# Large tiles at multiples of 2048 bytes in a partition of SBUF

## The chip, the cores and the metric

One NeuronCore of a Trainium2 chip runs the whole program in one launch. The metric is device time in microseconds. The kernel before takes 2143.19 us, the median of 3 runs (2142.52 to 2144.78). PE is TensorE, ACT is ScalarE, DVE is VectorE, POOL is GpSimd, SP is the engine that issues nearly all DMAs.

## The reference

The input is one sequence of 512 tokens of width 1024 and a context of 256 tokens, all in float32. A first block modulates both with adaptive layer norms (six vectors from `silu(c) @ w_ada`), multiplies by `w_in`, runs a bidirectional state space scan, a Fourier mix and a pooling mix, and multiplies by `w_out`. A feed-forward part follows:

```python
a = dwconv2d_grid(h @ w_up, conv_w, conv_b)      # w_up 1024 x 5632
val, gate = jnp.split(a, 2, axis=-1)
return (jax.nn.gelu(gate) * val) @ w_down        # w_down 2816 x 1024
```

Then come two hybrid layers. Each projects the normed stream (`w_in`), runs an attention over the best 256 keys of an indexer and a stabilised mLSTM, multiplies by `w_out`, and ends with

```python
u = rms_norm(h, g_mlp) @ w_ff1                   # 1024 x 4096
h = h + jnp.square(jax.nn.relu(u)) @ w_ff2       # 4096 x 1024
gate = jax.nn.sigmoid(rms_norm(h, g_ple) @ w_ple_gate + b_ple_gate)
return h + gate * (p_i @ w_ple)
```

## The kernel before, in words

**Layout.** Activations lie with features on the 128 partitions and tokens along the partition: a tile of 1024 features is 8 pieces of 512 float32, so 8 times 2048 bytes, 16,384 bytes in a partition. `h` is the residual stream, `mix` holds 8 working pieces, and `ring` has two slots of one weight tile each (1024 x 256, 8 pieces of 1024 bytes).

**Products.** A product is made at float32 accuracy from three matmuls in the float32r type. Each operand is held as a high and a low part: `xh`, `xl` for the activations that come out of a norm, `acts` for both parts of the activations inside the feed-forward parts (`U1`, `n.U`), of the input of `w_out_2` and of the gate projection, `ctxr` for the context, `wh`, `wl` for the weights. `product` (lines 794 to 796) and `part` (811 to 813) loop over the 8 pieces k of 128 contraction rows and issue `hi x hi`, `hi x lo`, `lo x hi`: stationary a 128x128 piece of `wh` or `wl` (512 bytes in a partition, the two halves of a tile 512 bytes apart, consecutive k 1024 bytes apart), moving a 128x512 piece of the activations. Every matmul loads its own weights first. `product_t` (828 to 830) turns it round: stationary a piece of `xh` or `xl`, moving 256 or 80 columns of `wh` or `wl`. All other matmuls (transposes, sums, Fourier, `w_ple`, attention) are in plain float32.

**Weights.** SP loads each tile into `ring` (line 741); ACT writes the high part into `wh` (line 1428), and DVE (1958) or POOL (2783) writes `ring - wh` into `wl`. The matmuls of a half wait for its low part. The order of all this in the mixers stands in the hand-written tables `MIXER` and `LAYER`; in the feed-forward parts the loops `up1`, `down1`, `up2`, `down2` set it. None of it depends on where a tile lies.

**Places.** `sb` opens an SBUF tensor; the allocator gives addresses in the order of the calls. The first tile begins at byte 1152 of each partition, and each later one at the next multiple of 32 after the one before it. So in the kernel before:

```
tile                         start (bytes)        past a multiple of 2048 / of 512
h                            1152                 1152 / 128
xh, xl                       17536, 33920         1152 / 128
wh, wl                       50304, 66688         1152 / 128
mix, ring                    83072, 99456         1152 / 128
small ones (con ... turn)    115840 to 133072     various
arena, acts, arena_f/m0/m1   133088 (the base)    2016 / 480
acts00, acts10 (n.U)         145376               2016 / 480
early                        172000               2016 / 480
ctxr, arena2                 198048               1440 / 416
```

The tiles from the base on overlap one another in time (they are opened and closed in `with` blocks): `arena` serves the first mixer, `acts` its feed-forward part, `arena_m` the mixer of a layer, `acts00` and so on its feed-forward part. `ahead` is opened only to push `early`, the landing place of seven weight tiles for the adaptive norm, above what the first norms use.

Of the kernel before, what the change touches and what calls it, by code (L numbers as in the profile page):

```python
# [9 lines left out]
I32 = mybir.dt.int32  # L10
# [21 lines left out]
def const_layout():  # L32
    names = [("ident", 128), ("ule", 128), ("uge", 128), ("ugt", 128), ("ult", 128), ("ones", 128),
             ("mean", 128), ("neg", 128), ("pen", 128), ("freq", 8), ("sel", 16), ("pair", 16), ("fold", 128)]
    at, n = {}, 0
    for name, w in names:
        at[name] = n
        n += w
    return at, n
# [57 lines left out]
def offsets(table):  # L97
    at, n = {}, 0
    for name, w in table:
        at[name] = n  # L100
        n += w
    return at, n
# [287 lines left out]
def build(nc, A, out):  # L390
    cat, cn = const_layout()
    pat, pn = offsets(PARAMS)
    rat, rn = offsets(ROWS)

    with ExitStack() as ctx:
        def sb(name, n, dt=F32, where=ctx):
            return where.enter_context(nc.sbuf_tensor(name, [128, n], dt))
# [8 lines left out]
        up, at, now = tally.up, tally.at, tally.now  # L406

        h_t, xh_t, xl_t = sb("h", 4096), sb("xh", 4096, F32R), sb("xl", 4096, F32R)
        wh_t, wl_t = sb("wh", 2 * SLOT, F32R), sb("wl", 2 * SLOT, F32R)  # L410
        mix_t, ring = sb("mix", 4096), sb("ring", NSLOT * SLOT)
        con, par, rb, mod = sb("con", cn), sb("par", pn), sb("rb", rn), sb("mod", 96)
        fw, pw, posi = sb("fw", 128), sb("pw", 128), sb("posi", 4, I32)
        rope, eps, csil_t, small = sb("rope", 64), sb("eps", 3), sb("csil", 256), sb("small", 1024)
        turn_t = sb("turn", 100)
        posf, ang, kk, rr = turn_t[:, 0:4], turn_t[:, 4:36], turn_t[:, 36:68], turn_t[:, 68:100]

        def by8(t):
# [3 lines left out]
        csil = csil_t[:, :].rearrange("p (k w) -> p k w", w=32)  # L422
# [48 lines left out]

        with ExitStack() as low:
            sb("ahead", 9728, where=low)
            early_t = sb("early", 7 * SLOT, where=low)
        early = {i: early_t[:, n * SLOT:n * SLOT + SLOT].rearrange("p (k n) -> p k n", k=8) for n, i in enumerate((0, 1, 4, 5, 2, 6, 7))}

        with ExitStack() as low:
            cut = Cut(sb("arena", 16240, where=low), 16240)
            arow = [cut(512), cut(512)]  # L480
            con1 = cut(1280)
            part2 = con1[:, 0:512]
            m1 = cut.o
            hc = cut(2048).rearrange("p (j t) -> p j t", j=8)
            xc_ctx = cut(2048).rearrange("p (j t) -> p j t", j=8)
            sq1, rs1, rs2, part1 = [cut(512) for _ in range(4)], cut(512), cut(256), cut(512)
            assert cut.o <= 9728
            cut.o = m1
            Xt = cut(3072).rearrange("p (q n) -> p q n", q=6)
            Bt = cut(1536).rearrange("p (q n) -> p q n", q=6)  # L490
            Z_ = cut(2048)
            Z = Z_.rearrange("p (q n) -> p q n", q=4)
            fA = Z_.rearrange("p (c i s f) -> p c i s f", c=4, i=2, s=2)
            BT = cut(1024).rearrange("p (g t) -> p g t", g=2)
            CT = cut(1024).rearrange("p (g t) -> p g t", g=2)
            acc = [cut(512) for _ in range(4)]
            Ms = [cut(1024) for _ in range(3)]
            with ExitStack() as high:
                ctxr = sb("ctxr", 4096, F32R, where=high)
                ch = ctxr[:, 0:2048].rearrange("p (j t) -> p j t", j=8)  # L500
                cl = ctxr[:, 2048:4096].rearrange("p (j t) -> p j t", j=8)
            with ExitStack() as high:
                cut = Cut(sb("arena2", 4096, where=high), 4096)
                pb = [cut(2 * 544).rearrange("p (i t) -> p i t", i=2) for _ in range(3)]
                cut.o = 0
                Sf = cut(2048).rearrange("p (q n) -> p q n", q=4)
                Sb = cut(2048).rearrange("p (q n) -> p q n", q=4)
                cut = Cut(sb("arena3", 3072, where=high), 3072)
                Ms.append(cut(1024))
                Ex, dmb = [cut(512), cut(512)], cut(512)  # L510
                dts, dtw0 = cut(256).rearrange("p (k n) -> p k n", n=32), cut(256)
# [12 lines left out]
        with ExitStack() as low:  # L524
# [3 lines left out]
            cut = Cut(sb("arena_f", 3584, where=low), 3584)  # L528
# [18 lines left out]
        for l in range(2):  # L547
            n = Layer()
            layers.append(n)
            with ExitStack() as low:  # L550
                cut = Cut(sb(f"arena_m{l}", 23824, where=low), 23824)
# [8 lines left out]
            with ExitStack() as low:  # L560
                cut = Cut(sb(f"arena_f{l}", 3072, where=low), 3072)
# [4 lines left out]
                with ExitStack() as high:  # L566
                    cut = Cut(sb(f"arena_p{l}", 5120, where=high), 5120)
# [2368 lines left out]
```

## Time and profile before

| | |
|---|---|
| median of 3 runs | 2143.19 us |
| the profiled execution, its own time | 2150.59 us |
| its span, first to last instruction | 2148.6 us |
| mean granted clock of TensorE | 0.981 |
| PE busy | 2084.7 us, 97% of the span |
| DVE, ACT, POOL busy | 54%, 41%, 37% |
| matmuls | 10,284 |
| DMA | 90 GB/s over the span |

How to read it: busy matmuls overlap one another, since they are pipelined. The duration of one (0.39 us for 512 columns) is its way through the array, and a new one starts well before the last has ended. How fast TensorE works is read from the distance between the starts of successive matmuls in a timeline, here called the pitch. 512 columns at 2.4 GHz are 213.3 ns, 256 columns 106.7 ns.

### The profile page before, as it was taken

Reading aid. Unit: us, or ns where it says so; the run is one execution under the profiler, and the core shown is the slowest. Engines: PE = TensorE matmul, PEld = TensorE weight load, DVE = VectorE, ACT = ScalarE, POOL = GpSimd, SP = SyncE. Lnnn points to the kernel's source line nnn. Section 1 sums busy time; section 2 is a strip of 40 time slices with the busy share of each in tenths; the row PEclk is TensorE's granted clock in tenths of the full one; section 3 lists DMA queues with packets and bytes.
Section 4 is the critical chain, followed back from the end, with each engine's and each line's share of the span. In section 5 each row is a group of like instructions: output and inputs, shape, how many; then the busy total and the mean of one; then the engine's idle time right before and its main releaser. Section 6 shows DMA issues by size and latency. Waiting matters only on the chain. (4 is left out here: it accounts for less than half of the span.)

```text
span 2148.6 us, 25815 instructions
## 1 busy us (share of the span) xinstructions
PE 2084.7 (97%) x10284; PEld 1608.4 (75%) x10284; DVE 1162.4 (54%) x2013; ACT 882.6 (41%) x1391; POOL 787.9 (37%) x404
## 2 busy tenths in 40 slices
PE   6999999999999999999999999989999999999998
PEld 3877677888887877667888887677776788888866
DVE  5366759995574579954523121345997553123124
ACT  4543334442333566854322122336677432222132
POOL 0233115675563334420544444001434134444420
PEclk9999999999999899999999999999999999999999
DMA  9134631232222202112333322221111133332212
GB/s 314 58 99 157 196 98 42 96 118 98 88 99 75 79 1 79 40 59 79 108 98 98 98 98 92 65 85 40 60 59 40 61 100 105 98 98 88 95 53 98
DMA packets 186662, 194.23 MB, mean 90 GB/s; under 512 B 8496, under 2 KB 181936, under 8 KB 186160
## 3 DMA queue, kind: packets, MB, share of 16 engines
q1 hardware_dynamic: 184880, 187.35, 27.1%
q10 hardware_dynamic: 1664, 5.24, 0.7%
q8 instruction: 82, 1.34, 0.3%
q14 instruction: 36, 0.29, 0.0%
HBM read 190.48 MB, written 2.10 MB: 90 GB/s over the span
## 5 line engine op out<-in xcount | busy, mean ns | idle before, releaser
L2783 POOL TENSOR_TENSOR wl<-ring,wh 128x1024 fp32r<-128x1024 f32 (+1 forms) x252 | 619.1, 2461 | 905.7 <-ACT wh L1428 904.7
L1428 ACT ACTIVATE wh<-ring 128x1024 fp32r<-128x1024 f32 (+2 forms) x294 | 304.4, 1043 | 348.6 <-PE ps L796 265.2
L794 PE MATMUL ps<-xh,wh 128*128 128x512 f32 x960 | 377.0, 393 | 1.9 <-POOL wl L2783 1.7
L795 PE MATMUL ps<-xl,wh 128*128 128x512 f32 x960 | 374.4, 390 | 0.0
L796 PE MATMUL ps<-xh,wl 128*128 128x512 f32 x960 | 374.1, 390 | 0.0
L794 PE MATMUL ps<-acts,wh 128*128 128x512 f32 x880 | 348.5, 396 | 3.1 <-DVE wl L1958 3.1
L796 PE MATMUL ps<-acts,wl 128*128 128x512 f32 x880 | 350.5, 398 | 0.0
L795 PE MATMUL ps<-acts,wh 128*128 128x512 f32 x880 | 347.7, 395 | 0.0
L2425 DVE SCALAR_TENSOR_TENSOR mix<-ps,par,mix 128x441 f32<-128x441 f32 (+2 forms) x352 | 213.6, 688 | 30.2 <-ACT mix L1659 30.1
L794 PEld LDWEIGHTS ps<-xh,wh 128*128 128x128 f32 x960 | 180.5, 188 | 45.6 <-issue 7.8
L795 PEld LDWEIGHTS ps<-xl,wh 128*128 128x128 f32 x960 | 180.6, 188 | 37.8 <-issue 0.7
L796 PEld LDWEIGHTS ps<-xh,wl 128*128 128x128 f32 x960 | 180.6, 188 | 37.8
L794 PEld LDWEIGHTS ps<-acts,wh 128*128 128x128 f32 x880 | 165.6, 188 | 50.0 <-issue 10.8
L795 PEld LDWEIGHTS ps<-acts,wh 128*128 128x128 f32 x880 | 165.5, 188 | 42.3 <-issue 0.7
L796 PEld LDWEIGHTS ps<-acts,wl 128*128 128x128 f32 x880 | 165.5, 188 | 38.6
L2496 DVE TENSOR_TENSOR h<-h,ps 128x512 f32<-128x512 f32 x64 | 44.1, 689 | 274.5 <-PE ps L796 274.5
L1726 ACT ACTIVATE acts<-mix 128x512 fp32r<-128x512 f32 x64 | 40.5, 632 | 235.3 <-DVE mix L2484 235.3
L2484 DVE SCALAR_TENSOR_TENSOR mix<-ps,arena_f 128x512 f32<-128x512 f32 x64 | 44.2, 690 | 142.0 <-PE ps L796 142.0
L828 PE MATMUL ps<-wh,xh 128*128 128x256 f32 (+1 forms) x352 | 109.3, 310 | 1.4 <-ACT arena_m L1433 1.1
L830 PE MATMUL ps<-wh,xl 128*128 128x256 f32 (+1 forms) x352 | 106.1, 302 | 0.0
L829 PE MATMUL ps<-wl,xh 128*128 128x256 f32 (+1 forms) x352 | 106.0, 301 | 0.0
L811 PE MATMUL ps<-xh,wh 128*128 128x512 f32 x224 | 95.9, 428 | 0.0
(431 smaller groups left out, 3141.4 us busy)
## 6 DMA issues: line engine op xcount, KB each, us to landing
ring<-in_w_ff_dram SPq DMA_DIRECT2D x64, 1024.0 KB, 5.4
ring<-in_w_in_dram SPq DMA_DIRECT2D x28, 1024.0 KB, 5.4
ring<-in_ffn_w_up_dram SPq DMA_DIRECT2D x22, 1024.0 KB, 5.0
ring<-in_w_ada_dram SPq DMA_DIRECT2D x17, 1024.0 KB, 5.2
ring<-in_w_out_dram SPq DMA_DIRECT2D x12, 1024.0 KB, 5.2
ring<-in_ffn_w_down_dram SPq DMA_DIRECT2D x8, 1024.0 KB, 5.0
ring<-in_w_ple_gate_dram SPq DMA_DIRECT2D x8, 1024.0 KB, 5.3
early<-in_w_ada_dram SPq DMA_DIRECT2D x7, 1024.0 KB, 12.1
```

The costliest lines, as they stand in the source:

```text
L794: t.matmul(b[0:m, 0:n], s.hi[:, k, a:a + m], x2[0][:, k, :], start=k == ks[0], stop=False)
L795: t.matmul(b[0:m, 0:n], s.hi[:, k, a:a + m], x2[1][:, k, :], start=False, stop=False)
L796: i = t.matmul(b[0:m, 0:n], s.lo[:, k, a:a + m], x2[0][:, k, :], start=False, stop=k == ks[-1])
L811: t.matmul(b[:, :], s.hi[:, k, a:a + 128], x2[0][:, k, :], start=k == ks[0], stop=False)
L828: t.matmul(b[:, 0:s.w], x0[:, k, :], s.hi[:, k, 0:s.w], start=k == 0, stop=False)
L829: t.matmul(b[:, 0:s.w], x0[:, k, :], s.lo[:, k, 0:s.w], start=False, stop=False)
L830: i = t.matmul(b[:, 0:s.w], x1[:, k, :], s.hi[:, k, 0:s.w], start=False, stop=k == 7)
L1428: a.activation(s.hi[:, :, c], s.ap[:, :, c], ACT.Copy).then_inc(*up("hi", "hi", name, hf))
L2425: k = v.scalar_tensor_tensor(o, grid(ps(key)[:, :], dr, dc, True), pc("ffn_conv_w", w * 44 + col), o, ALU.mult, ALU.add)
L2484: v.scalar_tensor_tensor(u, ps(key)[:, :], 0.0, n.rs2, ALU.max, ALU.mult).then_inc(*free(key))
L2496: v.tensor_tensor(h[:, j, :], h[:, j, :], ps(key)[:, :], ALU.add).then_inc(*free(key))
L2783: p.tensor_tensor(s.lo[:, :, c], s.ap[:, :, c], s.hi[:, :, c].bitcast(F32), ALU.subtract).then_inc(*up("lo_pool", "lo", name, hf))
```

## The change

The small tiles are opened first and the seven large ones after them. `turn` grows from 100 to 108 elements, which makes the small ones end at byte 18,416, rounded to 18,432, 9 times 2048. The large ones end at 133,120, 65 times 2048. As `ahead` and the arena have 32 bytes less room above them, `rs2` (256 elements, the reciprocal root of the context's variance) no longer has a place of its own in the arena and uses the first 256 elements of `small`, whose users begin later; `ahead` shrinks by 256 elements.

```diff
+        con, par, rb, mod = sb("con", cn), sb("par", pn), sb("rb", rn), sb("mod", 96)
+        fw, pw, posi = sb("fw", 128), sb("pw", 128), sb("posi", 4, I32)
+        rope, eps, csil_t, small = sb("rope", 64), sb("eps", 3), sb("csil", 256), sb("small", 1024)
+        turn_t = sb("turn", 108)
         h_t, xh_t, xl_t = sb("h", 4096), sb("xh", 4096, F32R), sb("xl", 4096, F32R)
         wh_t, wl_t = sb("wh", 2 * SLOT, F32R), sb("wl", 2 * SLOT, F32R)
         mix_t, ring = sb("mix", 4096), sb("ring", NSLOT * SLOT)
-        con, par, rb, mod = sb("con", cn), sb("par", pn), sb("rb", rn), sb("mod", 96)
-        fw, pw, posi = sb("fw", 128), sb("pw", 128), sb("posi", 4, I32)
-        rope, eps, csil_t, small = sb("rope", 64), sb("eps", 3), sb("csil", 256), sb("small", 1024)
-        turn_t = sb("turn", 100)
...
-            sb("ahead", 9728, where=low)
+            sb("ahead", 9472, where=low)
...
-            sq1, rs1, rs2, part1 = [cut(512) for _ in range(4)], cut(512), cut(256), cut(512)
-            assert cut.o <= 9728
+            sq1, rs1, rs2, part1 = [cut(512) for _ in range(4)], cut(512), small[:, 0:256], cut(512)
+            assert cut.o <= 9472
```

The places after it:

```
tile                         start (bytes)        past a multiple of 2048 / of 512
small ones (con ... turn)    1152 to 18416        various
h, xh, xl, wh, wl, mix, ring 18432 to 133120      0 / 0
arena, acts, arena_f/m0/m1   133120 (the base)    0 / 0
acts00, acts10 (n.U)         145408               0 / 0
early                        171008               1024 / 0
ctxr, arena2                 198080               1472 / 448
```

The instructions, their order, their waits and their shapes stay as they are.

## Rows read from the trace of the kernel before

**Rows 1.** The head of the page and its busy times by engine

```profile
span 2148.6 us, 25815 instructions
PE 2084.7 (97%) x10284; PEld 1608.4 (75%) x10284; DVE 1162.4 (54%) x2013; ACT 882.6 (41%) x1391; POOL 787.9 (37%) x404
```

**Rows 2.** Windows: length, busy us of PE, PEld, DVE, ACT, POOL, clock, DMA share, GB/s

```profile
449.75:500.00 50.25, 50.25 (x223) 41.63 (x222) 46.81 (x79) 21.70 (x28) 34.52 (x20) 1.00 0.28 91
1100.00:1130.00 30.00, 30.00 (x130) 24.12 (x130) 4.14 (x6) 6.05 (x6) 12.01 (x5) 1.00 0.28 82
```

**Rows 3.** Timeline of PE (start, duration), `xh` moving: two matmuls 27 starts apart

```profile
449.75 0.39 PE L794 MATMUL ps<-xh,wh 128*128 128x512 f32 x1
...
455.87 0.39 PE L794 MATMUL ps<-xh,wh 128*128 128x512 f32 x1
```

**Rows 4.** The same with `acts` moving: two matmuls 27 starts apart

```profile
1099.59 0.39 PE L794 MATMUL ps<-acts,wh 128*128 128x512 f32 x1
...
1105.89 0.39 PE L794 MATMUL ps<-acts,wh 128*128 128x512 f32 x1
```

**Rows 5.** The same with `ctxr` moving, 256 columns: two matmuls 33 starts apart

```profile
107.53 0.28 PE L794 MATMUL ps<-ctxr,wh 128*128 128x256 f32 x1
...
111.38 0.28 PE L794 MATMUL ps<-ctxr,wh 128*128 128x256 f32 x1
```

**Rows 6.** The same with weights moving, 256 columns: two matmuls 8 starts apart

```profile
177.53 0.28 PE L829 MATMUL ps<-wl,xh 128*128 128x256 f32 x1
...
178.49 0.28 PE L828 MATMUL ps<-wh,xh 128*128 128x256 f32 x1
```

**Rows 7.** Chain of waits: 28 plain float32 matmuls of 512 columns in a row

```profile
2086.38 12.02 PE ps L1223 x28
```

**Rows 8.** Timeline of PE where `acts` gives way to `xh`: 9 starts apart

```profile
1724.22 0.40 PE L794 MATMUL ps<-xh,wh 128*128 128x512 f32 x1
...
1726.30 0.39 PE L794 MATMUL ps<-xh,wh 128*128 128x512 f32 x1
```

**Rows 9.** Groups by form: count, busy us, mean ns, idle before and its releaser

```profile
L794 PE MATMUL ps<-xh,wh 128*128 128x512 f32 x960 | 377.0, 393 | 1.9 <-POOL wl L2783 1.7 <-DVE wl L1958 0.2
L794 PE MATMUL ps<-acts,wh 128*128 128x512 f32 x880 | 348.5, 396 | 3.1 <-DVE wl L1958 3.1
L811 PE MATMUL ps<-xh,wh 128*128 128x512 f32 x224 | 95.9, 428 | 0.0
L811 PE MATMUL ps<-acts,wh 128*128 128x512 f32 x64 | 27.0, 421 | 4.6 <-DVE acts L2771 4.6
L828 PE MATMUL ps<-wh,xh 128*128 128x256 f32 x288 | 87.0, 302 | 1.4 <-ACT arena_m L1433 1.1
L794 PE MATMUL ps<-ctxr,wh 128*128 128x256 f32 x48 | 13.4, 279 | 0.0
```

**Rows 10.** Groups by form of DVE, ACT and POOL, on tiles at different places

```profile
L2484 DVE SCALAR_TENSOR_TENSOR mix<-ps,arena_f 128x512 f32<-128x512 f32 x64 | 44.2, 690 | 142.0 <-PE ps L796 142.0
L2496 DVE TENSOR_TENSOR h<-h,ps 128x512 f32<-128x512 f32 x64 | 44.1, 689 | 274.5 <-PE ps L796 274.5
L1726 ACT ACTIVATE acts<-mix 128x512 fp32r<-128x512 f32 x64 | 40.5, 632 | 235.3 <-DVE mix L2484 235.3
L1448 ACT ACTIVATE arena_f<-h 128x512 f32<-128x512 f32 x40 | 25.3, 632 | 124.1 <-DVE h L2471 53.1 <-DVE h L2496 49.2 <-PE ps L896 11.3
L2783 POOL TENSOR_TENSOR wl<-ring,wh 128x1024 fp32r<-128x1024 f32 x244 | 604.3, 2481 | 882.9 <-ACT wh L1428 881.9
```

**Rows 11.** Waits of PE: us in total, times, longest

```profile
PE ps L877 <- DMA h<-in_x_dram: 10.8, 2, 8.5
PE ps L811 <- DVE acts L2771: 4.6, 2, 2.3
```

**Rows 12.** DMA issues: queue, count, KB each, median us to landing

```profile
arena_m<-in_w_iq_up_dram ACTq DMA_DIRECT2D x2, 512.0 KB, 3.9
mix<-in_p_dram ACTq DMA_DIRECT2D x2, 512.0 KB, 3.6
```

## The prediction, made blind

> **What bounds the kernel now.** I read the page's busy times first. PE is busy for 2084.7 us of 2148.6, 97% [rows 1], so only what PE does faster, or the 64 us in which it does nothing, can move the end. The windows come next: in a stretch of an up projection and in one of a down projection PE has no gap at all and the full clock, while POOL is busy for 34.5 of 50.25 us and for 12.0 of 30 us and DMA runs at under 30% [rows 2]. There nothing is late but PE itself. But "busy" doesn't say how fast a busy PE works, so the third view is the timeline, and in it the distance between starts. That is where this case lies, because a change of addresses alters no instruction, no order and no wait; it can act only through what one instruction takes.
>
> With `xh` or `xl` moving, 27 starts lie 6.12 us apart: 226.7 ns each [rows 3]. With `acts` moving, the same instruction on the same shape with the same kind of weights takes 6.30 us for 27: 233.3 ns [rows 4]. The columns alone would need 213.3 ns. So each matmul pays 13.3 ns above its columns in the first case and 20.0 ns in the second. The windows say the same by counts: 223 starts in 50.25 us are 225 ns each, 130 in 30 us are 231 ns, each a little low because a started matmul at the edge counts in full [rows 2]. The two differ in what other engines do at the same time (DVE 93% busy beside the cheap one, 14% beside the dear one), and the dear one is the quiet one, so the difference isn't contention with DVE, ACT or POOL. What is left that tells them apart is the place of the moving tile: `xh` begins 1152 bytes past a multiple of 2048, as `wh` and `wl` do, `acts` 2016 bytes past one.
>
> Three more rows fix how far that reasoning goes. Plain float32 matmuls of 512 columns take 12.02/28 = 429.3 ns [rows 7]; that is twice 213.3 and 2.6 ns, although these too load new weights each time. So plain float32 pays nothing for its place, and the extra is a matter of the float32r matmuls. With weights moving and `xh` stationary, 256 columns take 0.96/8 = 120.0 ns [rows 6], again 13.3 ns above the columns; there both tiles lie 1152 past, the roles are swapped and the length is halved, and the extra is the same. With `ctxr` moving, 1440 past, against `wh`, 256 columns take 3.85/33 = 116.7 ns [rows 5], an extra of 10.0 ns. So the extra is 13.3 where moving and stationary tile lie equally (0 bytes apart modulo 512), 20.0 at 352 apart and 10.0 at 288 apart. Within a stretch it does not change from k to k or half to half, though the stationary piece then steps by 512 and by 1024 bytes: whatever it depends on repeats every 512 bytes. I take this as a conflict between reading the moving operand and loading the next weights, which depends on how the two lie to one another.
>
> **The change part by part.** *The large tiles.* After the change `acts` and `wh`, `wl` lie 0 apart, as `xh` and `wh` do today, so the 233.3 ns should become 226.7 ns, 6.67 ns less. How many: 880 at each of three lines and 64 at each of three more, 944 x 3 = 2832 [rows 9]. 2832 x 6.67 ns = 18.9 us. All of them but a few stand where PE has no gap: the down projections, the gate projection and the second halves of `w_out_2`. The exception is the start of `w_out_2` in each layer, where PE waits for DVE's low parts, 4.6 us in two waits [rows 11]; of the first half's 48 matmuls per layer at most 96 x 6.67 ns = 0.6 us can vanish in such waits. I take off 0.2 us: 18.7 us. Where `acts` gives way to `xh` the first nine starts take 2.08 us and not 9 x 0.2267 = 2.04 [rows 8]; with both tiles alike this settling should go, five times 0.04 = 0.2 us (up after down, once in the first block and twice in each layer).
>
> *`xh`, `xl` against `wh`, `wl`*: both move by the same number of bytes, their relation stays, and I take 0. This is the largest unknown: (960 + 224) x 3 = 3552 matmuls of 512 columns and at least 288 x 3 = 864 of 256 [rows 9]. From below, if the place 0 costs no more than a plain float32 matmul (2.6 ns), each gains 10.7 ns, 47 us. From above, if 0 costs what 2016 costs, each loses 6.67 ns, 29 us. I take 0 since the four offsets that pieces of `wh` have today (128, 640, 1152, 1664) all cost the same.
>
> *`ctxr`*: 48 x 3 = 144 matmuls [rows 9]; its relation to `wh` goes from 288 to 448, which no row shows. Between 2.6 and 20.0 ns of extra where it is 10.0 now: -1.1 to +1.4 us; I take 0, the present value.
>
> *DVE, ACT, POOL*: DVE takes 690 ns with `arena_f` (2016 past) and 689 with `h` (1152 past), ACT 632 ns whether it writes `acts` or `arena_f` [rows 10]. The place costs these nothing: 0. PE's faster down projections ask for half a weight tile every 24 x 0.2267 = 5.44 us instead of 5.60; POOL makes one in 2.48 us [rows 10], so this supply doesn't turn late.
>
> *DMA*: destinations move too. The only pair of one size at two places is 512 KB into `arena_m`, 3.9 us, and into `mix`, 3.6 us [rows 12], 8% apart. The one wait of PE for a DMA is that for `h` at the start, 10.8 us [rows 11], and 8% of it is 0.9 us, so -0.9 to +0.9 us; I take 0, as the two rows are of different moments. Elsewhere weights arrive ahead.
>
> *`rs2` in `small`, `ahead`, `turn`*: the same instructions on other addresses; 0. There is no new wait, so nothing can queue behind one.
>
> Sum: -18.7 - 0.2 = -18.9 us. The profiled execution itself took 2150.59 us, 7.4 above the median of the runs; the same difference on the median gives 2143.19 - 18.9 = 2124.3 us. If only the relation counts, what is left open is `ctxr`, the start and the 0.6 us at `w_out_2`: 2121 to 2128.
>
> The Trainium skill has a rule against all this. "TensorE: Matmul & The Clock Gate", in "What happens when you issue a matmul", says that PE reads the moving operand and the next weights through two independent ports, and that loading weights takes no read bandwidth from the running matmul. By it the pitch can't depend on how the tiles lie, and the sum would be 0. The trace agrees for plain float32 (2.6 ns of extra) and disagrees with it as a whole for float32r, where the extra takes three values. The same page of the Trainium skill, section "Back-to-back issue gap", gives N/2.4 + 2.5 ns, 215.8 for 512 columns; none of the float32r streams here reaches it, and by it the time would be that of the deep fall among the rivals.
>
> **The rivals.** *The place doesn't matter (the change doesn't do what it says).* `acts` is also the only moving tile of 512 columns that lies above byte 131,072, and it does so after the change too. If the 20.0 ns come from that, or from anything else about `acts`, its pitch stays at 233.3 and the time within 1 or 2 us of 2143. For it: `ctxr` is up there too, and 20.0 ns on 512 columns and 10.0 on 256 are the same share, 9.4%. Against it: `xh` passes byte 32,768 and `wh` byte 65,536 on the way through their pieces, and rows 3 stay even. By the port rule of the Trainium skill's "TensorE: Matmul & The Clock Gate", quoted above, the time would be this one too.
>
> *Everything falls to what plain float32 pays.* If starts at 0 take the whole conflict away, 4416 matmuls gain 10.7 ns and the 2832 of `acts` gain 17.4: 47 + 49 = 96 us, 2047 us. For it: the extra does vary, so it isn't a fixed cost of float32r. Against it: with equal places today it is 13.3, not 0, in both roles.
>
> *The other side: the absolute place counts, and 0 is a bad one.* No row has a tile at 0; the nearest place modulo 2048 is 2016, 32 bytes before it, and it is the dear one. If `xh` takes over its 6.67 ns and `acts` keeps it, 4416 x 6.67 = 29.5 us are lost: 2172.7 us. It turns into a loss from the point where `xh` and its like lose more than 18.9 us/4416 = 4.3 ns each. Against it: places 512 apart cost the same, so 1152 stands for 128, and 2016 for 480; 0 then lies between them; and `ctxr`, off the multiples of 64 as `acts` is, is the cheapest of all.
>
> *In between*: `acts` improves, to some other value than 226.7, or `xh` shifts by 1 or 2 ns: 2128 to 2139.
>
> **How the numbers follow.** My forecast 0.65; no effect 0.12; everything falls 0.08; slower 0.10; in between 0.05. About 0.2%, 4.3 us, is what a measurement of this kernel can tell from no change. Faster by more: 0.65 + 0.08 + 0.05 = 0.78; within: 0.12; slower: 0.10. The time is the forecast's, 2124.3. Its own range of 2121 to 2128 holds not quite 0.65, so the range for 8 in 10 reaches over the middle to the case of no effect: 2119 to 2145, which leaves out the deep fall and the loss.
>
> **What would show it.** In the timeline of the changed kernel, 27 starts with `acts` moving should lie 6.12 us apart, and the nine after a change from `acts` to `xh` 2.04; with `xh` still 6.12; with `wh` moving 0.96 for 8; plain float32 still 12.02 for 28. DVE, ACT and POOL rows keep their means. I'm wrong in the step "relation, not place" if the `xh` streams move at all, and wrong altogether if `acts` stays at 6.30. If the pitches come out as said and the time doesn't fall by 17 us or more, the gain went into waits, first at `w_out_2` and the norms, and PE's share of the span would show it.

## The result, and the profile after

The kernel after takes 2130.68 us (median of 4 executions, 2129.14 to 2133.61) against 2143.99 (4 executions of the kernel before, 2142.52 to 2145.05): ratio 0.994, 95% interval 0.9923 to 0.9957. It is 13.3 us faster. Three later series of 5 and 6 executions, each beside the kernel before on the same chip, gave 0.9927, 0.9931 and 0.9917. The forecast was 2124.3 with a range of 2119 to 2145; the result lies in that range, but above the 2121 to 2128 that the prediction gave if only the relation counts.

The head of the page of the kernel after, against [rows 1]:

```profile
span 2129.5 us, 25815 instructions
PE 2061.1 (97%) x10284; PEld 1602.8 (75%) x10284; DVE 1161.6 (55%) x2013; ACT 882.1 (41%) x1391; POOL 787.1 (37%) x404
```

The span is 19.1 us shorter and PE's busy time 23.6, while DVE, ACT and POOL stay within 1 us: less work for PE, and not less waiting. Some 4 us of this pair are no gain of the change: the profiled execution before had a mean granted clock of 0.981, the one after 0.983 (0.002 of 2140 us, an estimate). PE's idle time even rises, from 63.9 to 68.4 us; part of that is the one execution profiled, since in further traces the waits listed for PE come to 61.3 and 61.9 us before and to 62.1 to 62.4 after. As before, the pitch tells more than the busy time. First the windows, to be read against [rows 2] (length, busy us of PE, PEld, DVE, ACT, POOL, clock, DMA share, GB/s). The second is again a stretch of a down projection:

```profile
449.75:500.00 50.25, 50.25 (x224) 41.60 (x223) 45.67 (x76) 20.01 (x27) 34.17 (x19) 1.00 0.31 104
1092.00:1122.00 30.00, 30.00 (x134) 24.82 (x134) 3.91 (x6) 6.15 (x6) 13.79 (x6) 1.00 0.35 105
```

In 30 us PE now starts 134 matmuls with `acts`, not 130; in the stretch with `xh` it starts 224, for 223 before. The timeline of the kernel after, pairs of matmuls 27 starts apart, first `xh`, then `acts`; then 33 starts of `ctxr`, 20 starts with weights moving, and the 9 starts where `acts` gives way to `xh`, against [rows 3 to 6, 8]:

```profile
449.83 0.39 PE L794 MATMUL ps<-xh,wh 128*128 128x512 f32 x1
...
455.95 0.39 PE L794 MATMUL ps<-xh,wh 128*128 128x512 f32 x1
...
1092.26 0.39 PE L794 MATMUL ps<-acts,wh 128*128 128x512 f32 x1
...
1098.38 0.39 PE L794 MATMUL ps<-acts,wh 128*128 128x512 f32 x1
```

```profile
105.02 0.28 PE L794 MATMUL ps<-ctxr,wh 128*128 128x256 f32 x1
...
108.91 0.28 PE L794 MATMUL ps<-ctxr,wh 128*128 128x256 f32 x1
...
175.13 0.28 PE L829 MATMUL ps<-wl,xh 128*128 128x256 f32 x1
...
177.53 0.28 PE L828 MATMUL ps<-wh,xh 128*128 128x256 f32 x1
```

```profile
1711.66 0.39 PE L794 MATMUL ps<-xh,wh 128*128 128x512 f32 x1
...
1713.70 0.39 PE L794 MATMUL ps<-xh,wh 128*128 128x512 f32 x1
```

`xh`: 6.12/27 = 226.7 ns, unchanged. `acts`: 6.12/27 = 226.7, where it was 233.3 [rows 4]. `ctxr`: 3.89/33 = 117.9, where it was 116.7 [rows 5]. Weights moving: 2.40/20 = 120.0, unchanged. The change from `acts` to `xh`: 2.04 us for 9, without the settling of [rows 8]. The chain of waits of the kernel after shows the plain float32 stream at its old 12.02 us for 28 [rows 7]:

```profile
2068.57 12.02 PE ps L1223 x28
```

Groups by form (count, busy us, mean ns, idle before and its releaser), against [rows 9, 10]:

```profile
L794 PE MATMUL ps<-xh,wh 128*128 128x512 f32 x960 | 376.8, 392 | 1.9 <-POOL wl L2783 1.7 <-DVE wl L1958 0.2
L794 PE MATMUL ps<-acts,wh 128*128 128x512 f32 x880 | 345.3, 392 | 3.3 <-DVE wl L1958 3.3
L794 PE MATMUL ps<-ctxr,wh 128*128 128x256 f32 x48 | 13.5, 281 | 0.0
L2484 DVE SCALAR_TENSOR_TENSOR mix<-ps,arena_f 128x512 f32<-128x512 f32 x64 | 44.2, 690 | 141.9 <-PE ps L796 141.8
```

The `acts` group is 3.2 us less busy and `xh`'s 0.2. Busy time of a group is no measure of the pitch, since the matmuls overlap, but it moves where the pitch does. Waits of PE (us in total, times, longest), against [rows 11]:

```profile
PE ps L877 <- DMA h<-in_x_dram: 10.8, 2, 8.6
PE ps L896 <- ACT arena_f L1448: 7.4, 4, 3.6
PE ps L811 <- DVE acts L2771: 4.6, 2, 2.3
```

The one wait that grows in every pair of traces is the middle one, PE for ACT's squares in the norms: 6.3 to 6.7 us in the kernels with slow `acts`, 7.2 to 7.8 in those with fast ones. Most of the growth stands around the gate projection of layer 0 (2.7 us before, 3.2 to 3.4 after), where PE now comes sooner and ACT doesn't. That gives back about 1 us.

The windows of the start, 14 to 38 us, of the kernel before and then of the kernel after (same columns as above), show what no step had foreseen:

```profile
14.00:38.00 24.00, 19.58 (x127) 7.20 (x127) 15.62 (x22) 14.96 (x29) 4.67 (x2) 1.00 1.10 342
```

```profile
14.00:38.00 24.00, 18.87 (x133) 7.24 (x130) 17.13 (x24) 15.45 (x30) 4.68 (x2) 1.00 1.09 380
```

At the same share of busy DMA engines 380 GB/s arrive, not 342. Issues of 1 MB into `ring` (the 64 of `w_ff`) land in 5.2 us, not 5.4, those into `early` in 10.8, not 12.1. Of [rows 12], the 512 KB into `mix` still take 3.6, and those into `arena_m` 4.2 where they took 3.9; but in the further traces these last take 4.2 before and 3.9 to 4.2 after, so that pair of rows is scatter.

### The profile page after: what moved, and what is told of

Its sections match the earlier page's. It is cut to its first block and busy times, and to the rows that moved or that the text cites. A ratio compares the mean times of both kernels' runs of the same rounds, so it can differ in the third digit from the quotient of the medians.

```text
span 2129.5 us, 25815 instructions
## 1 busy us (share of the span) xinstructions
PE 2061.1 (97%) x10284; PEld 1602.8 (75%) x10284; DVE 1161.6 (55%) x2013; ACT 882.1 (41%) x1391; POOL 787.1 (37%) x404
## 5 line engine op out<-in xcount | busy, mean ns | idle before, releaser
L794 PE MATMUL ps<-acts,wh 128*128 128x512 f32 x880 | 345.3, 392 | 3.3 <-DVE wl L1958 3.3
L796 PE MATMUL ps<-acts,wl 128*128 128x512 f32 x880 | 342.7, 389 | 0.0
L795 PE MATMUL ps<-acts,wh 128*128 128x512 f32 x880 | 342.6, 389 | 0.0
L794 PEld LDWEIGHTS ps<-acts,wh 128*128 128x128 f32 x880 | 165.4, 188 | 45.5 <-issue 11.6
## 6 DMA issues: line engine op xcount, KB each, us to landing
early<-in_w_ada_dram SPq DMA_DIRECT2D x7, 1024.0 KB, 10.8
```

Of the source, the lines that this page charges most:

```text
L794: t.matmul(b[0:m, 0:n], s.hi[:, k, a:a + m], x2[0][:, k, :], start=k == ks[0], stop=False)
L795: t.matmul(b[0:m, 0:n], s.hi[:, k, a:a + m], x2[1][:, k, :], start=False, stop=False)
L796: i = t.matmul(b[0:m, 0:n], s.lo[:, k, a:a + m], x2[0][:, k, :], start=False, stop=k == ks[-1])
```

## The experiments

### A map of the pitch by addresses

One kernel with nothing but streams of 24 matmuls, each line at another start of the moving tile (m) and the stationary one (s), counted in elements of 4 bytes in the code and in bytes in the text:

```diff
+for i in range(24): t.matmul(P[1][:, 0:512], W[:, s + 256 * (i % 8):s + 128 + 256 * (i % 8)],
+                             X[:, m + 512 * (i % 8):m + 512 + 512 * (i % 8)], start=i == 0, stop=i == 23)
```

> This kernel leaves the whole computation out and writes x back. It runs streams of 24 float32r matmuls, each stream on a line of its own, and varies only where the stationary piece begins (s bytes past a multiple of 2048) and where the moving piece begins (m bytes past one): 16 values of m in steps of 32 bytes with s = 0 and 512 columns; the same 16 differences m - s with s = 128; the same with s = 0 and 256 columns; m = 4 to 48 bytes; s = m = 4 to 256; plain float32 at m = 0, 32, 128. Before that, 4 MB are loaded in four DMAs of 1 MB to destinations 0, 32, 64, 128, 256 and again 0 bytes past a multiple of 2048. Theory 1, the relation counts: the 16 pitches with s = 0 and with s = 128 are the same row by row, 226.7 ns at difference 0 and 233.3 ns at 352 (480 against 128), 116.7 ns for 256 columns at 288, and s = m gives 226.7 at any value. Theory 2, the place of the moving tile alone counts: the row with s = 0 and the row with s = 128 agree by m and not by m - s; 233.3 at m = 480, 226.7 at m = 0 and 128, and 233.3 at s = m = 32. Plain float32 gives 429.3 ns everywhere by both. DMA: if the jump from 348 to 386 GB/s at the start is a matter of the destination, the groups at 0 and 256 run near 386 GB/s and those at 32, 64 and 128 near 348; if it isn't, all six are alike.

The chain of waits of this run (start, us, engine, line). Lines 152 to 167 are s = 0 and m = 0, 32, ..., 480 bytes; 168 and 169 the first two again with the stationary tile at 128; 184 to 191 are 256 columns at 0, 32, ..., 224 bytes:

```profile
119.11 5.44 PE ps L152 x24
124.55 5.60 PE ps L153 x24
130.16 5.50 PE ps L154 x24
...
163.69 5.47 PE ps L160 x24
...
208.29 5.48 PE ps L168 x24
213.77 5.60 PE ps L169 x24
...
297.50 2.87 PE ps L184 x24
300.37 2.83 PE ps L185 x24
...
314.57 2.73 PE ps L190 x24
...
409.47 20.60 PE ps L212 x48
```

A row's total divided by 24 is a little too high where the relation has just changed, since the first few starts of such a stream are slower (up to 236 ns in line 160, then 226.7). From the seventh start on the pitch is, by the distance of the moving start past the stationary one, to some 0.2 ns:

```
bytes past      0      32     64     96     128    160    192    224
512 columns     226.7  233.3  228.8  233.4  233.6  234.2  233.2  233.3   ns
256 columns     119.8  117.8  117.7  120.0  118.8  117.5  113.4  118.2   ns
```

The same run moved 4 MB by DMA to destinations 0, 32, 64, 128, 256 and again 0 bytes past a multiple of 2048 (windows of each group; the last column is GB/s):

```profile
22.18:34.00 11.82, 0.00 (x0) 0.00 (x0) 0.00 (x0) 0.00 (x0) 1.00 1.02 355
36.00:48.20 12.20, 0.00 (x0) 0.00 (x0) 0.00 (x0) 0.00 (x0) 1.00 1.03 333
...
64.00:76.70 12.70, 0.00 (x0) 0.00 (x0) 0.00 (x0) 0.00 (x0) 1.00 1.02 326
78.50:89.80 11.30, 0.00 (x0) 0.00 (x0) 0.00 (x0) 0.00 (x0) 1.00 1.02 362
```

Destinations on a multiple of 256 get 355 to 362 GB/s, those at 32, 64 and 128 get 326 to 333. From the first packet of a group to its last the trace has 11.6 to 11.8 us for the one kind and 12.6 to 12.8 for the other. That fits the faster start of the kernel after, whose `ring` and `early` came to multiples of 256. The rates that I had expected, 386 and 348, were those of a shorter stretch of the kernel's start.

### All large tiles at 2016, and the two kernels again

The kernel before, with four small tiles opened first and padded, so that `h`, `xh`, `xl`, `wh`, `wl`, `mix` and `ring` come to 2016 past a multiple of 2048, where `acts` lies: the relation of the kernel after, the dear place of the kernel before, and none of its DMA gain.

```diff
+        mod, turn_t, posi, eps = sb("mod", 96), sb("turn", 104), sb("posi", 8, I32)[:, 0:4], sb("eps", 8)[:, 0:3]
         h_t, xh_t, xl_t = sb("h", 4096), sb("xh", 4096, F32R), sb("xl", 4096, F32R)
...
-        con, par, rb, mod = sb("con", cn), sb("par", pn), sb("rb", rn), sb("mod", 96)
+        con, par, rb = sb("con", cn), sb("par", pn), sb("rb", rn)
```

> The kernel before with four small tiles (mod, turn, posi, eps: 864 bytes) opened ahead of the large ones and the rest behind them, so that xh, xl, wh, wl, mix and ring begin 2016 bytes past a multiple of 2048, where acts already is; the arena keeps its place at 133088. Nothing is at a multiple of 2048 and nothing at a multiple of 64. Theory 1, the relation of moving and stationary tile counts: acts falls from 233.3 to 226.7 ns, xh stays at 226.7, and the time is that of the changed kernel but for DMA. Theory 2, each tile's own place counts: acts stays at 233.3 and xh rises to 233.3 ns, 29 us slower than before, some 2172 us. DMA: by the destination theory the ring's and early's loads stay at the slower rate, 348 GB/s in the first 40 us.

> The changed kernel again, five rounds against the kernel before on the same chip. The trace shows 18.6 us less in the pitches of acts, but the medians lay only 13.3 us apart. If the profiled execution of before was merely one with more clock gating than usual, the ratio stays at 0.994; if the four runs of the first timing were unlucky, it goes to 0.9912 (18.9 us of 2143). Theory 1 for the missing 5 us: waits in the mixers between engines, which the trace after shows 3.7 us longer, are there in every execution.

> The kernel before again, for a second profile. If its first profiled execution (2150.6 us against a median of 2143.2) was one with more time at the lower clock, this one lies at 2143 to 2146 us with less time at it, and its pitches are 226.7 and 233.3 ns again.

Measured: 2133.36 us, ratio 0.9933 (0.9913 to 0.9953); beside it the kernel after 2131.67, 0.9927 (0.9909 to 0.9944). The one execution of the kernel before gave 2148.95, above the 2143 to 2146 expected, and its old pitches. The ratio of the kernel after, 0.9927, lies between the two values that its expectation had. Timeline of the shifted kernel, 27 starts apart, and its window of the start:

```profile
1094.00 0.39 PE L794 MATMUL ps<-acts,wh 128*128 128x512 f32 x1
...
1100.12 0.39 PE L794 MATMUL ps<-acts,wh 128*128 128x512 f32 x1
```

```profile
14.00:38.00 24.00, 19.60 (x126) 7.23 (x125) 15.62 (x22) 14.96 (x29) 4.66 (x2) 1.00 1.10 340
```

6.12/27 = 226.7 ns with everything at the place that I had called possibly bad, and 340 GB/s. Place 0 isn't needed, and the DMA rate isn't either: within the interval the whole gain comes without both. The rival "absolute place" falls.

### Only the relation of acts spoiled

The kernel after with 32 bytes in front of each `acts`, nothing else:

```diff
+            sb("gap_a", 8, where=low)
...
+                sb(f"gap_a{l}", 8, where=low)
```

> The changed kernel with eight elements (32 bytes) opened ahead of acts, acts00 and acts10, so that these lie 32 bytes past a multiple of 2048 and all else stays where the change put it, the DMAs' destinations too. By the relation theory acts goes back to 233.4 ns (the map's row at difference 32) and xh stays at 226.7; the time is 18.7 us above that of the changed kernel on the same chip. If the shortfall of the measured gain against the pitches is something that the faster acts brings with it, this kernel is only some 15 us slower; if it comes from the other tiles' new places, this kernel is the full 18.7 us slower and lies 3 us above the kernel before.

> The changed kernel again, for the comparison with the one above on the same chip and for more executions: a ratio of 0.9927, and at equal granted clock 17.5 us below the kernel before.

> The kernel before against itself: a ratio of 1.000, whose interval shows what five rounds can tell. Its executions scatter over 10 us with the granted clock, 2143 to 2145 us at 0.985 and 2148 at 0.984. If the mean clock of the executions is 0.9845 here and 0.983 for the changed kernel, the missing 2 to 4 us lie in the clock and not in the work.

Measured: 2145.79 us, ratio 0.9997 (0.9988 to 1.0007); beside it the kernel after 2131.8, 0.9931 (0.9917 to 0.9946), and the kernel before against itself 1.0001 (0.9988 to 1.0015). Timeline and start window of the spoiled kernel, whose line 796 is line 794 of the others:

```profile
1094.07 0.39 PE L796 MATMUL ps<-acts,wh 128*128 128x512 f32 x1
...
1100.36 0.40 PE L796 MATMUL ps<-acts,wh 128*128 128x512 f32 x1
```

```profile
14.00:38.00 24.00, 18.86 (x135) 7.40 (x131) 17.29 (x25) 15.29 (x30) 4.67 (x2) 1.00 1.10 381
```

6.29/27 = 233 ns, and the gain is gone altogether, with the DMA at its fast 381 GB/s. With the run before it this is a table of two by two: fast `acts` and slow DMA give 0.9933, slow `acts` and fast DMA give 0.9997. The change is worth what the relation of `acts` to the weights is worth; anything else in it is below what these runs can tell, 1 to 2 us. The spoiled kernel lies 14.0 us above the kernel after, not 18.7: the branch of the expectation by which the shortfall against the pitches comes with the faster `acts`, and not with the other tiles' new places.

### Which matmuls care

Streams as in the products of this kernel (hi x hi, lo x hi, hi x lo from separate tiles), then turned round with weights moving, with 32 to 96 stationary columns, with 384 and 128 moving ones, and in bfloat16. The start of the moving tile is again the only thing changed from line to line.

```diff
+for i in range(24): t.matmul(P[0][0:M, 0:N], (WH, WH, WL)[i % 3][:, 256 * (i // 3):256 * (i // 3) + M],
+                             (XH, XL, XH)[i % 3][:, m + 512 * (i // 3):m + N + 512 * (i // 3)], start=i == 0, stop=i == 23)
```

> This kernel leaves the whole computation out and writes x back. It runs streams of 24 matmuls with the kernel's own order (high x high, high x low, low x high, over 8 pieces) and varies the difference r between the place of the moving and of the stationary tile. Expected from the first map: with 512 columns 226.7 ns at r = 0, some 228.7 at 64 and 233 to 234 at all others. With 256 columns, weights stationary, the context's case: 116.7 ns at 32 (as in the kernel before, 288 apart) and 117.8 at 192 (as in the changed one, 448 apart), although the first map, with an order in which the piece changes at each matmul, had 117.8 and 113.4; so the order counts too. With activations stationary and 256 columns of weights moving: 120.0 at r = 0; if r = 192 gives 113.4 here, a layout for the token-major products is worth 6.6 ns on 864 matmuls. If the extra comes from reading the next weights beside the moving operand, a stationary piece of 32 or 64 columns pays less of it than one of 128, at r = 0 and at r = 96; if it comes from the moving read alone, the width of the stationary piece changes nothing. With 384 columns moving the extra is the same in ns as with 512 by the first, and three quarters of it by the second. bfloat16: no extra at any r by both, since it reads half the bytes.

The chain of waits: 512 columns at 0 and 96 past; weights moving at 0 and 192; 32 stationary columns at 0 and 96; 384 moving ones at 0 and 96; bfloat16 at 0:

```profile
53.14 5.44 PE ps L141 x24
...
69.69 5.61 PE ps L144 x24
...
120.33 2.87 PE ps L157 x24
...
137.40 2.73 PE ps L163 x24
...
142.96 5.56 PE ps L165 x24
148.52 5.59 PE ps L166 x24
...
176.25 4.19 PE ps L171 x24
180.44 4.24 PE ps L172 x24
...
189.99 5.20 PE ps L175 x24
```

From start to start, settled: 226.7 and 233.3; 120.0 and 113.3; 231.7 and 233.2; 173.3 and 176.8; bfloat16 215.8 at each of the three distances tried. So bfloat16, like plain float32, pays nothing for its place; of the three types only float32r does. With 128 moving columns a float32r matmul takes 111.7 ns at 0 and at 96, more than twice its columns (53.3 ns) and without an effect of place. The order of the three products doesn't matter, against what I expected: 256 columns in the kernel's order take 117.8 ns at 32 and 113.4 at 192, as in the first map. What the mechanism is stays open. My picture was that reading the moving operand collides with loading the next weights. Against it: a stationary tile of 32 columns, a quarter of the load, makes the cheap relation dearer (231.7) and the dear one no cheaper (233.2); 64 and 96 columns take 230 ns at 0 and 231 at 96, so there is no order by the size of the load. At 96 bytes the extra above the columns grows with their number (13.3 ns at 256, 16.8 at 384, 20.0 at 512), at 0 it is 13.3 at all three.

### Above byte 131,072, and the step between pieces

`acts` and `ctxr` lie in the upper part of the memory and `ctxr`'s pieces are 1024 bytes apart, so 256 columns were streamed with the moving tile low and high, the stationary one low and high, and pieces 1024 and 2048 apart; then 512 columns from a high tile.

```diff
+XF, WF = sb("XF", 5120, F32R), sb("WF", 5120, F32R)   # bytes 133,120 and 153,600
+for i in range(24): t.matmul(P[0][:, 0:256], WH[:, 256 * (i // 3):256 * (i // 3) + 128],
+                             XF[:, m + 256 * (i // 3):m + 256 + 256 * (i // 3)], start=i == 0, stop=i == 23)
```

> Leaves the whole computation out (the output is the input written back). It streams 256 and 512 float32r columns with the moving start 0, 32, ..., 224 bytes past the stationary start modulo 256, once with both tiles low in memory, once with the moving tile above byte 131,072, once with both above it, and once with the moving pieces 2,048 instead of 1,024 bytes apart. Theory 'relation alone': height and stride change nothing; 256 columns repeat 119.8, 117.7, 117.7, 120.0, 118.8, 117.5, 113.3, 118.3 ns in every group, and 512 columns 226.7 at 0, 228.8 at 64 and 233 to 234 elsewhere. Then the 117.8 ns of the kernel after's rotation inputs at relation 192 needs another reason. Rival 'the upper part of the memory': streams whose moving tile lies above byte 131,072 cost more at every relation (233.3 at 512 columns even at relation 0, and 117 to 120 instead of 113.3 at relation 192). Rival 'stride': 113.3 at relation 192 comes only with one of the two strides.

The chain of waits: at 192 past, both low (146), moving high (154), pieces 2048 apart (170); 512 columns from a high tile at 0 and 32 (172, 173):

```profile
62.18 2.73 PE ps L146 x24
...
84.81 2.73 PE ps L154 x24
...
130.08 2.73 PE ps L170 x24
...
135.64 5.49 PE ps L172 x24
141.13 5.60 PE ps L173 x24
```

The four groups of eight lines, both tiles high among them, are the same to 0.2 ns in pitch. Line 172 settles at 226.7 ns like the low tiles. Neither height nor stride matters; with it the rival "it is something about `acts`, above 131,072" is refuted directly, as it already was by the kernel with everything at 2016. One oddity stays: `ctxr` lies 32 bytes past the weights modulo 256 in the kernel before and 192 in the kernel after, for which the maps have 117.8 and 113.4 ns; the traces have 116.7 and 117.9. I don't know why. It is 0.2 us in all.

### Where the last 3 us went

The pitches give 18.9 us, the first medians 13.3 and the three later series 14 to 18. The executions carry their mean granted clock with them, so I sorted the 21 of the kernel after and the 62 of the kernel before from the four later series (means in us, count in brackets; "all" holds one more of the kernel before at 0.981 and four at 0.986):

```
clock           0.982         0.983        0.984         0.985         all
before          2152.3 (10)   2149.4 (9)   2147.5 (11)   2144.5 (27)   2147.1 (62), mean clock 0.9841
after           2132.2 (12)   2132.0 (2)   2129.9 (6)    2126.8 (1)    2131.3 (21), mean clock 0.9828
```

At one clock the two kernels are 17.4 to 17.7 us apart (0.983 to 0.985; 20.2 at 0.982), over all 15.8. The difference in mean clock, 0.0013 of 2140 us, is 2.8 us, an estimate. The kernel with `acts` 32 bytes on had 0.9846 (12 executions) and that with everything at 2016 had 0.9828 (6): the lower clock goes with the fast `acts`, not with the addresses. In each of the three series with both kernels the kernel after has the lower mean, by 0.0007 to 0.0021. The clock is granted down mainly in the two mixers (a granted clock of 0.93 to 0.95 from 680 to 960 and from 1380 to 1680 us, PE busy for 266 of 280 us in the first; 1.00 in the products between and behind them). Two runs asked whether it matters when they begin. Filler, plain float32 matmuls, ahead of each:

```diff
+                if key in (("dn", 1, 0), ("ff2", 0, 1, 0)):
+                    spin(b, 8 if key[0] == "dn" else 18)
```

> The kernel after with 8 and 18 filler matmuls in plain fp32 (429.2 ns each, 3.43 and 7.7 us) ahead of the last products before the mixers of layers 0 and 1, so that each mixer begins about as late as in the kernel before. Theory 'the granted clock falls differently because the mixers begin earlier': the mean granted clock returns from 0.983 to about 0.9845, which is worth 2 to 3 us, and the time is that of the kernel after plus 11.2 less 2 to 3: 2140 to 2141. Rival 'a faster stream is gated more, whenever it comes' (or 'by chance'): the clock stays at 0.983 and the time is 2142.5 to 2143.5. Rival 'filler ahead of the mixer keeps the clock up in it': the clock goes above 0.9845 and the time is below 2139.

> The kernel after once more, on the chip of the run above. By the mean of the executions so far: 2131.1 +- 0.8, ratio 0.993, granted clock 0.983. If the clock of the executions were an accident of the chip and not of the kernel, it comes at 0.984 to 0.985 here and the time at 2127 to 2129.

Measured: 2152.17 us (11 executions, mean 2152.6 +- 0.6), mean clock 0.9843. I had counted the filler wrong. Each call of `spin` comes to two matmuls in the trace, 10,336 against 10,284, 52 x 429.2 ns = 22.3 us instead of 11.2. The kernel after, beside it: 2131.28, ratio 0.9917 (0.9904 to 0.9931), mean 2131.7, clock 0.9826. So with the filler taken off the run took 2152.6 - 22.3 = 2130.3, 1.4 us less than the kernel after, and the clock did come back. But by the filler the first mixer began 6.9 us later than in the kernel after and the second 22.3 (7.1 and 22.6 in the two traces of that series), not 3.4 and 11.2. The next run has 4 and 9 in place of 8 and 18:

> The run with filler ahead of the mixers, mended: there every filler matmul came to two of 429.2 ns, 22.3 us in all. Here 4 and 9 of them, so 8 x 429.2 ns = 3.4 us ahead of the mixer of layer 0 and 18 x 429.2 ns = 7.7 us ahead of layer 1's, which then begin as late as in the kernel before; the sum is 11.2 us. Theory 'it matters when the mixer begins': mean granted clock 0.984 to 0.985, like that of the kernel before, and a mean of 2139.5 to 2141. Rival 'no relation, the clock of an execution is chance': mean clock 0.983 and a mean of 2131.3 + 11.2 = 2142.5, 2141.5 to 2143.5.

Measured: 2141.31 us (9 executions, mean 2141.6 +- 0.9), ratio 0.9976 (0.9962 to 0.9989), mean clock 0.9831. With 11.2 us of filler taken off that is 2130.4, 0.9 +- 1 below the kernel after. Its mixers' first matmuls stand at 700.4 and 1426.9 us, those of the kernel before in three traces at 700.6 to 707.9 and 1424.2 to 1431.7. The clock is not the 0.984 to 0.985 that the theory asked for, and the time just above its 2139.5 to 2141. So this run speaks against the moment at which the mixers begin, but the run before it, with the mixers later still, had the clock back at 0.9843; the two together leave it unsettled. That the granted clock is lower with fast `acts` is measured in the four kernels without filler; through what, is open.

## Why the prediction was right, and where it was off

*"The difference isn't contention, it is the place."* Right, by the table of two by two.

*"Relation, not place."* Right: `xh` did not move, `acts` came to its 226.7 ns, and everything at 2016 is as good as everything at 0. The period was taken too long: 256 bytes, not 512. It did no harm, since the change makes the distance 0 by either. The picture behind it, a conflict between reading the moving operand and loading the next weights, is not borne out: fewer stationary columns made the cheap relation dearer (231.7 ns at 32). That the relation was the right thing to change was reasoned from three values of the extra; why the relation counts wasn't known and still isn't.

*`acts`, 2832 x 6.67 ns = 18.9.* The pitch is as said. Summed over all distances between starts with `acts` moving, the first pair of traces differs by 18.6 us, two further pairs by 17.1 and 18.7.

*0.2 us lost in waits.* Too small: the waits at `w_out_2` stayed at 4.6 us [rows 11], but PE's wait for ACT's squares grew by 1 us, and I had not looked for it. Here the faster stretch ended against an engine that wasn't faster.

*Settling, 0.2 us.* Right, 2.04 us for nine starts, but `acts` gives way to `xh` seven times in the traces, not five: 0.3 us.

*`xh`, `xl`: 0, between -47 and +29.* Right. *`ctxr`: 0.* 144 x 1.2 ns = +0.2 us. *DVE, ACT, POOL: 0.* Right, 690 ns as in [rows 10].

*DMA: 0, between -0.9 and +0.9.* The effect exists, 342 to 380 GB/s at the start, and is worth nothing measurable, as the wait for `h` is still 10.8 us. The rows that I bounded it by said nothing: `mix` takes 3.6 at either place, and `arena_m` scatters between 3.9 and 4.2 at either.

*"The same difference on the median."* This is the step that was off. It carries the sum over to the three executions of the kernel before, whose median, 2143.19, lay 3.9 below the mean of 62. With 1.0 for the wait and 2.8 for the clock that makes 7.7; the measured mean of 2131.3 is 7.0 above the forecast of 2124.3, the first median 6.4. The result left the 2121 to 2128 of the forecast's own case and fell where the rival "in between" stood, 2128 to 2139 with a chance of 0.05, without its mechanism: `acts` went to 226.7 and `xh` didn't shift. The range held because it reached to the case of no effect, which was caution about other things and no knowledge of this one. The sign "if the time doesn't fall by 17 us, the gain went into waits" was wrong in the main too: about 1 us went there.

The Trainium skill's rule in "TensorE: Matmul & The Clock Gate", "What happens when you issue a matmul", that moving operand and next weights come through independent ports, would have had no effect of place here. These runs agree with it for bfloat16 (215.8 ns at three places) and plain float32 (429.2 at three), and not for float32r. The section "Back-to-back issue gap" of the same page of the Trainium skill gives 215.8 ns for 512 columns, which the bfloat16 streams match and no float32r stream reaches. It calls this the gap of an isolated matmul and gives about 131 ns for a stream of weight loads and matmuls of 512 columns; no stream of 512 columns here comes below 215.8.

## What to carry to other kernels

Before tuning a TensorE-bound kernel further, read the pitch of each stream, not its busy time: here two streams of one shape differed by 3% in something that cost nothing to mend. For 512 moving columns of float32r let the moving tile begin at the same byte modulo 256 as the stationary one, each on a multiple of 32; for 256 columns that is among the dearest relations by the map (see below), and it has to be measured in the kernel. Let DMA destinations begin on a multiple of 256; that was worth nothing measurable here, but the rate in the map was some 8% higher. Expect less in time than the pitches say: some of it comes back as a wait for the next engine and as granted clock.
